# A hybrid attention, delta-net and expert block on one core: transfers and ScalarE work reordered, lengths by a matrix of ones, beta and decay in column groups

## The reference

```python
h = rms_norm(x, norm_mix_gain)
(dq, dk, dv, gq, gk, gv, g_beta, g_dec, g_gate, m_gate_a, m_gate_b) = split(h @ w_in)
# attention: softmax per head and half, chunk-causal mask
a = p[:, :, 0] - lam * p[:, :, 1];  y_a = rms_norm(a @ dv, gain) * (1 - lambda_init)
# gated delta net, 4 heads of 128, chunks of 64
q, k, v = split(silu(causal_depthwise_conv([gq, gk, gv], conv_w)))
q = q * rsqrt(sum(q*q) + EPS) * 128 ** -0.5;  k = k * rsqrt(sum(k*k) + EPS)
beta = sigmoid(g_beta);  g = -exp(a_log) * softplus(g_dec + dt_bias)
gcum = cumsum(g within a chunk);  decay_mat = exp(gcum_i - gcum_j), causal
a_low = strict_lower((k * beta) @ k.T * decay_mat)
u, w = solve(eye + a_low, [v * beta, k * beta * exp(gcum)])
intra = (q @ k.T) * decay_mat
# scan over the 4 chunks
v_new = u - w @ S;  o = (q * exp(gcum)) @ S + intra @ v_new
S = S * exp(gcum_last) + (k * exp(gcum_last - gcum)).T @ v_new
y_b = rms_norm(o, gain) * silu(g_gate)
merged = sigmoid(m_gate_a) * (y_a @ w_branch_attn) + sigmoid(m_gate_b) * (y_b @ w_branch_gdn)
x = x + merged @ w_out;  x = x + hier_moe(rms_norm(x));  return rms_norm(x)
```

## Time and profile before

| what | value |
|---|---|
| median of 3 runs | 524.45 us (524.1 to 526.62) |
| the profiled execution's own time | 524.34 us |
| its span, first to last instruction | 522.6 us |
| TensorE busy, weight loads busy | 468.3 us (90%), 356.8 us (68%) |
| VectorE busy | 194.5 us (37%) |
| ScalarE busy | 123.0 us (24%) |
| GpSimd busy | 13.5 us (3%) |
| mean granted clock of TensorE | 0.947 of full speed |
| share of the chain that ended last | TensorE 68%, DMA 21%, DVE 4%, ACT 2% |
| moved by DMA | 136.82 MB, mean 262 GB/s |

### The profile page before, as it was taken

How to read it: one execution, slowest core, us unless ns; L and a number is a source line. 1 busy time by engine, 2 the same in 40 slices (tenths; PEclk the granted TensorE clock), 3 DMA queues, 4 the chain that set the end, 5 groups by cost and what they waited for, 6 DMA issues and landing times.

```text
span 522.6 us, 10447 instructions
## 1 busy us (share of the span) xinstructions
PE 468.3 (90%) x4429; PEld 356.8 (68%) x4429; DVE 194.5 (37%) x556; ACT 123.0 (24%) x310; POOL 13.5 (3%) x40
## 2 busy tenths in 40 slices
PE   8999999994996995999999989999997779768694
PEld 7884989873695885988874557776775465636451
DVE  1275128844332343343131155344433231413323
ACT  4001133100103006032001263333322121212235
POOL 6011000000000000000000000000000000000000
PEclk9999999998998898999999989999999887978798
DMA  8549469254132104044339867999999999999982
GB/s 319 128 156 395 155 255 388 61 190 150 28 136 101 61 0 162 0 162 161 126 137 423 361 241 290 421 419 417 421 418 421 421 418 421 420 421 417 418 347 87
DMA packets 37266, 136.82 MB, mean 262 GB/s; under 512 B 8480, under 2 KB 9952, under 8 KB 24928
## 3 DMA queue, kind: packets, MB, share of 16 engines
q1 hardware_dynamic: 29008, 134.26, 64.4%
q10 hardware_dynamic: 8064, 1.32, 1.4%
q0 software_dynamic: 144, 0.52, 0.3%
HBM read 134.39 MB, written 1.70 MB: 260 GB/s over the span
## 4 chain that ended last, share of the span: by engine, by line
PE 68%; DMA 21%; DVE 4%; ACT 2%; issue 2%; SPq 1%; ACTq 0%; DVEq 0%
PE ps L828 25%; DMA arena<-in_moe_w_up 11%; PE ps L1155 9%; DMA ring<-in_moe_w_up 5%; PE ps L1062 5%; PE ps L1047 5%; PE ps L845 4%; PE ps L1124 4%; PE ps L1186 3%; PE ps L1176 3%; PE ps L1164 2%; DMA arena<-in_w_in 2%; DMA arena<-stored_A 2%; DMA stored_inverses<-arena 1%; PE ps L993 1%
## 5 line engine op out<-in xcount | busy, mean ns | idle before, releaser
L828 PE MATMUL ps<-arena 128*128 128x256 f32 (+1 forms) x640 | 161.4, 406 | 1.0 <-DMA arena<-in_w_in 1.0
L828 PEld LDWEIGHTS ps<-arena 128*128 128x128 f32 x640 | 119.9, 192 | 29.3 <-issue 15.8
L1155 PE MATMUL ps<-arena 128*32 128x128 f32 x1088 | 43.0, 300 | 14.4 <-DMA arena<-in_moe_w_up 13.9
L1155 PEld LDWEIGHTS ps<-arena 128*32 128x32 f32 x1088 | 33.0, 117 | 23.2 <-DMA arena<-in_moe_w_up 16.3
L1155 PE MATMUL ps<-ring,arena 128*32 128x128 f32 x960 | 37.0, 296 | 8.7 <-DMA ring<-in_moe_w_up 8.6
L1155 PEld LDWEIGHTS ps<-ring,arena 128*32 128x32 f32 x960 | 28.5, 115 | 16.1 <-DMA ring<-in_moe_w_up 10.4
L642 ACT ACTIVATE arena<-ps 32x256 f32<-32x256 f32 x64 | 24.1, 377 | 58.3 <-PE ps L1176 57.8
L1186 PE MATMUL ps<-arena,rw 128*128 128x512 f32 x64 | 32.2, 648 | 1.1 <-DVE arena L1794 1.1
L1124 PEld LDWEIGHTS ps<-arena 128*128 128x128 f32 x256 | 29.3, 192 | 3.3 <-issue 3.3
L1124 PE MATMUL ps<-arena 128*128 128x128 f32 x256 | 30.8, 279 | 0.8 <-DVE arena L1721 0.8
L1794 DVE COPY arena<-ps 32x256 f32<-32x256 f32 x64 | 26.7, 417 | 11.4 <-PE ps L1176 10.2
(11 more groups left out here) (259 smaller groups left out, 464.8 us busy)
## 6 DMA issues: line engine op xcount, KB each, us to landing
arena<-in_w_in SPq DMA_DIRECT2D x9, 2048.0 KB, 8.0
arena<-in_moe_w_gate SPq DMA_DIRECT2D x17, 1024.0 KB, 25.8
arena<-in_moe_w_up SPq DMA_DIRECT2D x17, 1024.0 KB, 26.2
arena<-in_moe_w_down SPq DMA_DIRECT2D x17, 1024.0 KB, 25.9
ring<-in_moe_w_gate SPq DMA_DIRECT2D x15, 1024.0 KB, 25.0
ring<-in_moe_w_up SPq DMA_DIRECT2D x15, 1024.0 KB, 26.3
ring<-in_moe_w_down SPq DMA_DIRECT2D x15, 1024.0 KB, 26.0
arena<-in_w_out SPq DMA_DIRECT2D x2, 2048.0 KB, 8.0
```

The lines of the kernel that those rows point to most:

```text
L828: last = pe.matmul(out, lhs, rhs, start=(k == 0), stop=(k == KD - 1))
L1155: last = pe.matmul(c.ps[ROWS * q:ROWS * (q + 1), i % 2, 0:P], c.Hg[par][:, k, ROWS * i:ROWS * (i + 1)], c.gu_w[slot][:, :, k, start:start ...
```

## The change

1. SP: the first half of gk's weights comes in one transfer instead of two, and TensorE makes the first half of all four parts of gk before the second half of any. dq's load no longer waits for bd. dv's load waits for the blocks of A (`blocks_loaded`) instead of the store of A; ma0's load waits for the strips of the inverses (`inverse_loaded`).
2. Beta and decay: eight products with 32 columns of weights in four column groups (bdT, k and k + 4 in the same group), copied by ScalarE, then two products with `pick8`, which sum the groups and turn them.
3. Lengths: two products 128x512 each for k (ssk) and q (ssq) with the full matrix of ones, so that every partition gets the sum; ScalarE takes the root of 128x1024, VectorE the reciprocal of 128x1024 and the product with ck or cq. ss, rnk and rnq are gone.
4. gsum: both tiles of tokens in one product, 4 products instead of 8.
5. ScalarE: ma0 is copied after the first exponentials, ma1 after the second.

```diff
@@ SIDE
-SIDE = [("consts", 1), ("bd", 1), ("ss", 1), ("rnk", 1), ("rnq", 1), ("gsum", 1), ("grow", 1), ("gram", 1),
+SIDE = [("consts", 1), ("bdT", 1), ("ssk", 1), ("bd", 1), ("ssq", 1), ("gsum", 1), ("grow", 1), ("gram", 1),
@@ load_chunk (SP)
         if i == CI["dv"]:
-            sp.wait_ge(s["A_stored"], 16)
+            sp.wait_ge(s["blocks_loaded"], 16)
+        if i == CI["ma0"]:
+            sp.wait_ge(s["inverse_loaded"], 32)
@@ scalar_program
+    act.wait_ge(s["side_ready"], SI["bdT"] + 1)
+    act.activation(c.bdT, c.side[side_pair("bdT")][:, 0:TOK], ACT.Copy).then_inc(s["bdT_ready"], 1)
...
+        act.activation(dst.rearrange("p h f -> p (h f)"), c.side[side_pair(name)], ACT.Sqrt, bias=c.eps).then_inc(s["lengths_root"], 1)
+        act.wait_ge(s["lengths_root"], n)
+        act.sem_inc(s[f"side_free{side_pair(name)}"], 1)
+    lengths("ssk", c.sqk, 1)
...
     act.activation(c.lam[:, 2:4], c.lam[:, 0:2], ACT.Exp).then_inc(s["lam_exp"], 1)
+    lengths("ssq", c.sqq, 2)
@@ scalar_program
     take_T(4)
-    evacuate("ma0", c.mg[0], "mg_ready", ACT.Sigmoid)
...
-    evacuate("ma1", c.mg[1], "mg_ready", ACT.Sigmoid)
+    evacuate("ma0", c.mg[0], "mg_ready", ACT.Sigmoid)
...
     exps(1)
+    evacuate("ma1", c.mg[1], "mg_ready", ACT.Sigmoid)
@@ tensor_program
+        for j in range(2):
+            last = pe.matmul(blk(ps, j, 512), c.ones, squares[:, 2 * j:2 * j + 2, :].rearrange("p h f -> p (h f)"), start=True, stop=True)
...
+        q = k % 4
+        last = pe.matmul(ps[ROWS * q:ROWS * (q + 1), 0:TOK], wbd[:, k, 0:ROWS], c.hT[:, k, :], start=(k < 4), stop=(k >= 4))
...
+        last = pe.matmul(c.side[side_pair("bd")][:, 512 * t:512 * t + 8], c.bdT[:, t * P:(t + 1) * P], c.pick8, start=True, stop=True)
...
+    for j, mask in enumerate((c.upper, c.chunk, c.half0, c.half1)):
+        last = pe.matmul(ps[:, 8 * j:8 * j + 8], mask, c.g, start=True, stop=True)
@@ vector_program
+    v.wait_ge(s["lengths_root"], 1)
+    v.reciprocal(c.sqk, c.sqk).then_inc(s["lengths_inverse"], 1)
+    v.wait_ge(s["lengths_inverse"], 1)
+    v.tensor_tensor(c.ck, c.ck, c.sqk, ALU.mult).then_inc(s["k_normed"], 1)
...
+    v.wait_ge(s["lengths_root"], 2)
+    v.reciprocal(c.sqq, c.sqq).then_inc(s["lengths_inverse"], 1)
+    v.wait_ge(s["lengths_inverse"], 2)
+    v.scalar_tensor_tensor(out=c.cq, in0=c.cq, scalar=float(P) ** -0.5, in1=c.sqq, op0=ALU.mult, op1=ALU.mult).then_inc(s["q_normed"], 1)
```

More of the change, by code:

```diff
@@ L292, in load_chunk @@
             k0 = KD // 2
-            for k in range(0, k0, 2):
-                sp.dma_start(dst[:, k:k + 2, :], w_in[:, k:k + 2, col:col + n]).then_inc(s[f"first_loaded{k // 2}"], 16)
+            sp.dma_start(dst[:, 0:k0, :], w_in[:, 0:k0, col:col + n]).then_inc(s["first_loaded"], 16)
         sp.dma_start(dst[:, k0:, :], w_in[:, k0:, col:col + n]).then_inc(s[f"stage_loaded{i % 2}"], 16)
@@ L817, in project @@
                 pe.wait_ge(s["hU_odd" if k // 2 % 2 else "hU_even"], 2 * (k // 4) + 2)
-                if k < KD // 2 and k % 2 == 0:
-                    pe.wait_ge(s[f"first_loaded{k // 2}"], 16)
+                if k == 0:
+                    pe.wait_ge(s["first_loaded"], 16)
                 elif k == KD // 2:
@@ L827, in project @@
                 out, lhs, rhs = blk(c.pair[i % 2], part, 512), c.hT[:, k, part * P:(part + 1) * P], w[:, k, n - 512:n]
-            last = pe.matmul(out, lhs, rhs, start=(k == 0), stop=(k == KD - 1))
+            last = pe.matmul(out, lhs, rhs, start=(k == 0 and (i > 0 or part % 2 == 0)), stop=(k == KD - 1),
+                             skip_group_check=(i == 0))
             if between:
@@ L849, in tile @@
         return ap[:, h, t * P:(t + 1) * P]
-    project("gk", 0)
+    for b in range(4):
+        project("gk", b, range(KD // 2))
     turn_lengths()
-    for b in range(1, 4):
-        project("gk", b)
+    for b in range(4):
+        project("gk", b, range(KD // 2, KD))
     for b in range(4):
         project("gq", b)
-    project("bdg", 0)
-    project("bdg", 1)
     i = CI["bdg"]
     wbd = c.stage[i % 2][:, 0:KD * 520].rearrange("p (k n) -> p k n", k=KD)
-    side("bd")
[L864 to L869, removed]
@@ L870, in tensor_program @@
-    project("gv", 0, between=beta_and_decay)
-    project("gv", 1)
[L873 to L883, removed]
@@ L885, in tensor_program, with lengths @@
-    pe.wait_ge(s["rn_ready"], 1)
-    for j, name in enumerate(("rnk", "rnq")):
-        each(name, lambda t, h, j=j: c.rn[:, 8 * j + 4 * t + h:8 * j + 4 * t + h + 1].to_broadcast([P, P]), lambda t, h: c.ident)
+    def lengths(name, squares, n):
+        ps = side(name)
+        pe.wait_ge(s["masks_ready"], 1)
+        pe.wait_ge(s["squares_ready"], n)
+        for j in range(2):
+            last = pe.matmul(blk(ps, j, 512), c.ones, squares[:, 2 * j:2 * j + 2, :].rearrange("p h f -> p (h f)"), start=True, stop=True)
+        last.then_inc(s["side_ready"], 1)
@@ new lines, in tensor_program @@
+    project("bdg", 0)
+    ps = side("bdT")
+    for k in range(KD):
+        q = k % 4
+        last = pe.matmul(ps[ROWS * q:ROWS * (q + 1), 0:TOK], wbd[:, k, 0:ROWS], c.hT[:, k, :], start=(k < 4), stop=(k >= 4))
+    last.then_inc(s["side_ready"], 1)
+    project("bdg", 1)
+    lengths("ssk", c.sqk, 1)
+    project("gv", 0)
+    side("bd")
+    pe.wait_ge(s["bdT_ready"], 1)
+    pe.wait_ge(s["pick8_ready"], 1)
+    for t in range(NT):
+        last = pe.matmul(c.side[side_pair("bd")][:, 512 * t:512 * t + 8], c.bdT[:, t * P:(t + 1) * P], c.pick8, start=True, stop=True)
@@ L888, in tensor_program @@
+    last.then_inc(s["side_ready"], 1)
+    project("gv", 1)
+    lengths("ssq", c.sqq, 2)
+    project("gv", 2)
     project("gv", 3)
@@ L1432, in vector_program @@
     last.then_inc(s["g_ready"], 1)
[L1434 to L1444, removed]
+    v.wait_ge(s["lengths_root"], 2)
+    v.reciprocal(c.sqq, c.sqq).then_inc(s["lengths_inverse"], 1)
+    v.wait_ge(s["lengths_inverse"], 2)
+    v.scalar_tensor_tensor(out=c.cq, in0=c.cq, scalar=float(P) ** -0.5, in1=c.sqq, op0=ALU.mult, op1=ALU.mult).then_inc(s["q_normed"], 1)
+    v.wait_ge(s["q_normed"], 1)
     ps = side("gsum")
@@ L1629, in new_state @@
                 for h in range(H):
-                    chain(v.scalar_tensor_tensor(out=c.S[:, h, :], in0=c.S[:, h, :], scalar=col(c.sums_exp, 16 + 4 * n_ + h),
+                    chain(v.scalar_tensor_tensor(out=c.S[:, h, :], in0=c.S[:, h, :], scalar=col(c.sums_exp, 16 + 8 * (n_ % 2) + 4 * (n_ // 2) + h),
                                                  in1=blk(ps, H + h), op0=ALU.mult, op1=ALU.add))
```

26 lines of the change are left out of this document (10 added, 16 removed).

## The result

| | before | after |
|---|---|---|
| median | 525.54 us (4 runs, 524.1 to 526.95) | 503.56 us (4 runs, 501.58 to 507.13) |
| ratio, 95% interval | | 0.959 (0.953 to 0.965) |
| the profiled execution, its span | 524.34, 522.6 us | 503.65, 501.9 us |
| mean granted clock | 0.947 | 0.961 |

The account below looks back on a forecast made before the run. Up to 270 us TensorE's chain was taken to bound the kernel, with gaps of 6.6, 5.9 and 4.2 us that lower its clock. 6.6 + 2.5 - 2.0 + 6.05 + 7.0 = 20.1 us off 524.34: 504.2 us, range 499 to 509.

Parts of the forecast that it names:

- TensorE's products: Before the decay rows: fewer small products; TensorE would be through with the decay rows at 72.3 instead of 81.05 us.
- rival (c): Wide reciprocal as cheap as a product, VectorE no longer holds TensorE: A ready at 90.2, 495.8 us; chance 0.05.
- The wide reciprocals: Two VectorE reciprocals over 128x1024 ahead of the decay rows, 6.55 us each, for which TensorE will wait.
- (a): Wide reciprocals cost nearly a third more per element, 2.05 us more each: 508.3 us; chance 0.09.
- (d): Reciprocal with no fixed part worth the name: 16.3 us gives 523.7, 26.1 us gives 543; chance 0.03.
- A ready at 96.65: End of A, after the decay rows' subtractions: ready at 96.65 us instead of 98.91.
- Rival (b): The blocks' 8.4 us are their own, from 1024 small runs, not the neighbour's: 508.1 us; chance 0.07.
- The store behind dk's copy: On ScalarE the inverses' store waits for dk's copy, taking 2.9 of 5.4 us; first level still 6.6 us earlier.
- 2.0 lost: In ktok and dk: a 3.8 us gap before ktok brings TensorE's clock down, 2.0 us lost (bounds 0 and 2.6).
- 2.5 gained: At the inverse's first level: TensorE's gap falls from 6.6 to 2.2 us; if its clock stays up, 2.5 us gained.
- Exponentials first: ScalarE's exponentials before the copies of ma0 and ma1: 6.05 us gained to the first probabilities' turn, 7.0 at the second place.
- Rival (e): Another wait (the probabilities' turn, the maxima) holds the second exponentials; the 7.0 us are gone, 511.2 us; chance 0.04.

Follow-up runs that it names:

- SP's waits alone: The kernel before with only SP's two new waits (dv's load for the blocks, ma0's for the inverses' strips): 517.62 us, ratio 0.989 to before.
- the constant: The kernel after with each wide reciprocal replaced by a multiplication of the same elements with 1/45: 495.24 us, ratio 0.945 to before.
- exponentials alone: The kernel before with only ScalarE's new order, ma0 and ma1 copied behind the exponentials: 512.72 us, ratio 0.977 to before.
- reciprocals twice: The kernel after with a second reciprocal of the same width, into memory nobody reads, ahead of each wide one: 515.23 us, ratio 0.982 to before.
- dv's load at the store: The kernel after with dv's load released by the store of A again, ma0's wait kept: 506.17 us, ratio 0.963 to before.

## Why the prediction was right, point by point

- **TensorE's products.** Without VectorE's reciprocals in the way ktok begins at 90.2 to 90.4 us (three executions); the prediction had 90.2 for rival (c). The price list of the earlier trace rows held.
- **The wide reciprocals.** 6.55 us each was taken from two steps of 50 and 38 ns between narrow ones; 6.55 was measured. The rows of after, by shape (busy, mean ns | idle before, releaser):

```profile
L1442 DVE RECIPROCAL arena<-arena 128x1024 f32<-128x1024 f32 x1 | 6.6, 6553 | 3.5 <-ACT arena L504 3.5
...
L1411 DVE RECIPROCAL arena<-arena 128x1024 f32<-128x1024 f32 x1 | 6.6, 6552 | 1.6 <-ACT arena L504 1.6
```

  Rivals (a) and (d) fall with it. The repeat count of 8 that the Trainium skill gives for reciprocal (VectorE: DVE Perf Modes, the 8-slice pipeline, "First, the fixed hardware budget") came to 8.5 us as an estimate; the measurement, 6.4 ns per element over all, decides against it here. That both lie in line ahead of A is shown by doubling them (ktok 13.1 us later) and by taking them away (rival (c)'s 495.8, measured 495.24).
- **A ready at 96.65:** 96.57. TensorE idle 2.9 and 3.8 us: 2.8 and 3.5.
- **The blocks.** 3.0 us alone was forecast; 3.1 was measured, and 2.7 to 3.4 in the other runs with nothing beside them. With dv's load beside them they take 9.33 and 9.55. Rival (b), that they are slow by themselves, falls. The two waits cost nothing elsewhere: dv's load leaves at 103.05 (forecast 103.1), and no wait for dv's or ma0's weights stands in TensorE's list.
- **The store behind dk's copy.** The wait that was to take 2.9 of the 5.4 us is there, grown to 5.0 us by the half clock in dk (the store leaves at 115.27 instead of 110.28), and its removal brings back the 1.1 us of TensorE's last gap and no more.
- **The store of the inverses was mis-sized:** 3.2 taken from A's, 2.37 measured, and 2.36 with SP's waits alone. The loads with their issue took 3.1 instead of 3.4. Together with a half clock that cost 0.3 us less than forecast (next point) and some tenths, that is 1.6 us more gained up to the first level than the sum had: that level starts at 122.01, where the sum had 123.6 (121.6 and the 2.0 lost).
- **The clock.** 2.0 lost behind ktok: the products behind it take 5.14 us where the full clock takes 3.46, so 1.7. Ktok itself takes 1.09, but that is what it takes behind a wait at the full clock too (SP's waits alone, the constant). 2.5 gained at the first level: the two pieces take 5.49 instead of 7.69 us, so 2.2, because the first product of the level follows a short wait and costs 2.05 rather than 1.78. Whether the clock stays up there went with the gap in every execution profiled: behind 1.0 or 1.1 us (five of them) it stayed up, behind 4.4 to 6.6 us (five) it did not.
- **Exponentials first.** 6.05 forecast to the turn, 5.75 in the trace; 7.0 behind it, 5.25 + 1.4 = 6.65. The 0.3 missing at the turn is the last products before it, which take 2.04 us behind a short wait instead of the 1.75 forecast. The idle times left, 0.9 and 0.5, were measured at 0.9 and 0.7. Rival (e) falls: the second exponentials start as soon as the maxima are there. ScalarE's timeline of after at that place, the table's load and its wait for the maxima (L1576):

```profile
178.85 1.28 ACT L567 ACT_TABLE_LOAD   x1 [18.34 <-DVE small L1576]
180.15 0.47 ACT L567 ACTIVATE arena<-ps,small 128x256 f32<-128x256 f32 x1
```

- **The sum:** 20.1 forecast, 20.7 between the profiled executions. The terms that missed (first level with its clock +1.3, exponentials -0.65) go against each other, so that the sum came this near is in part luck. The forecast of 504.2 is 0.6 over both the profiled time and the median. The median of before rose by 1.1 us with its fourth run, so by medians 22.0 us were gained, 1.9 over the forecast, and the agreement of the two absolute times looks better than that of the gains.
- **Slips that changed nothing.** The prediction removes two small reciprocals where the rows have one; its chain does not use the number. Rival (b)'s 125.5 and 508.1 need a store of 4.8 us: with its own 3.2 the level starts at 123.8, which gives 506.4. The lower end of the forecast's own range, 499.5, has no terms: no clock drop and a store of 2.5 give 501.5, and faster blocks cannot add to that, since the store waits for dk's copy.

Where my expectations of the runs were off by more than a microsecond (exponentials alone 1.4, reciprocals twice 1.6, dv's load at the store 1.2), the traces have the half clock each time: it fell between 70 and 80 us, where it had not been counted; it fell into a wait, where it cost nothing; and it was left out behind a longer gap. Ma0's load without its wait took 509.37 us where I had 506, or 508.5 with the clock: the store beside it took 6.49 us and not 4.8. Open is what draws it in one execution and not in the next, and why one run of after took 507.13 us.

## What to carry to other kernels

A small transfer on the chain of waits should have no large load beside it: two waits on the queue of the large loads, which had slack, made two small transfers two to three times as fast and brought 7.3 us, some 2 of them by the clock that then stayed up. Which shared part slows them, the queues, their engines or the memory, no run here tells. When a wait is removed, look at what the instruction stands behind on its own engine (here the copy of dk), and order each engine's program by who is waited for, not by what is ready first: two copies moved behind the exponentials brought 12 us. Work moved from TensorE to VectorE in a wider shape is paid there in full when it lies ahead of the next product; price it per element from two narrow rows, and ask whether an idle engine has a cheaper form of it.

## What the runs showed of the hardware that was not expected

- Reciprocal on VectorE has no cheaper price for width: 166, 204 and 254 ns for 2, 8 and 16 elements, 6552 ns for 1024. A product with a constant over the same shape takes 0.69 us, ScalarE's Ln 1.11 and Exp 1.06.
- 64 KB gathered in runs of 64 bytes land in 2.7 to 3.4 us alone and in 8.3 to 9.6 beside one load of 2 MB on another queue; a store of 128 KB takes 2.4 alone and 4.8 to 6.5 beside such a load.
- The same gaps of TensorE in the same program brought the lower clock at different places in different executions; it cost 1.7 us behind ktok, where TensorE's work was the chain, 2.2 to 2.9 at the first level, and nothing where a wait followed.
